# The samples' state step rebuilt and moved to blocks 1 and 2, and the state stores split into two groups

## What is computed

```python
def wkv7_scan(S0, r, w, k, v, kk, a):
    def step(S, inp):
        r_t, w_t, k_t, v_t, kk_t, a_t = inp
        sa = jnp.einsum('bhij,bhj->bhi', S, -kk_t)
        S = (S * w_t[:, :, None, :] + sa[..., None] * (kk_t * a_t)[:, :, None, :]
             + v_t[..., None] * k_t[:, :, None, :])
        return S, jnp.einsum('bhij,bhj->bhi', S, r_t)
    xs = tuple(jnp.moveaxis(t, 1, 0) for t in (r, w, k, v, kk, a))
    S, ys = lax.scan(step, S0, xs)
    return jnp.moveaxis(ys, 0, 1), S
...
    y_prompt, p_new = run_trunk(x_prompt, p_states, W, 0)      # state starts at zero
    y_sample, s_new = run_trunk(x_sample, s_states, W, PAST_LEN)  # state S0 is an input
```

## Time and profile before

| | us |
|---|---|
| median of three runs | 1320.65 (1320.16 to 1322.43) |
| the profiled execution's own time | 1319.88 |
| its span in the profile | 1318.1 |
| TensorE busy | 1212.6, 92% of the span |
| VectorE, ACT, POOL busy | 607.2, 333.7, 161.6 |
| mean granted clock of TensorE | 0.928 of full speed |

### The profile page before, as it was taken

The page is one execution under the profiler, slowest core; times in us unless marked ns, Lnnn a source line. Parts: engine busy times, 40 slices in busy tenths (PEclk is TensorE's granted clock), DMA queues, the critical chain, the costliest instruction groups (busy, mean ns, idle before and its releaser), DMA issues.

```text
span 1318.1 us, 22066 instructions
## 1 busy us (share of the span) xinstructions
PE 1212.6 (92%) x9190; PEld 1162.3 (88%) x9190; DVE 607.2 (46%) x886; ACT 333.7 (25%) x488; POOL 161.6 (12%) x134
## 2 busy tenths in 40 slices
PE   6999999999997899938789899969999999999994
PEld 6999999999997899937677758969999999999993
DVE  4443334333435768746644421466343334333445
ACT  5322122111213433102333211224221222212121
POOL 0000000000001303699700000031000000000002
PEclk9999999999998799977989856978999999999996
DMA  5222222222212022282010000212222222222211
GB/s 220 97 96 80 85 91 95 76 84 96 88 60 76 32 65 81 66 57 37 1 33 1 1 0 1 60 56 65 96 95 81 80 95 87 78 90 96 74 54 68
DMA packets 34364, 92.13 MB, mean 70 GB/s; under 512 B 10496, under 2 KB 10880, under 8 KB 34176
## 3 DMA queue, kind: packets, MB, share of 16 engines
q1 hardware_dynamic: 32576, 87.26, 22.4%
q10 hardware_dynamic: 1728, 4.03, 0.8%
HBM read 87.99 MB, written 3.28 MB: 69 GB/s over the span
## 4 chain that ended last, share of the span: by engine, by line
PE 87%; DVE 9%; DMA 1%; issue 1%; ACT 1%; ACTq 0%; SPq 0%; POOL 0%; DVEq 0%
PE ps L293 24%; PE ps L295 24%; PE ps L294 23%; DVE tb L424 2%; PE ps L781 2%; PE ps L780 1%; DMA raw<-in_w_out 1%; DVE xl L385 1%; PE ps L756 1%; PE ps L772 1%; PE ps L315 1%; PE ps L817 1%; PE ps L824 1%; PE ps L309 1%; DVE tb L416 1%
## 5 line engine op out<-in xcount | busy, mean ns | idle before, releaser
L293 PE MATMUL ps<-xh,wh 128*128 128x272 f32 x1840 | 544.0, 296 | 32.5 <-DVE xl L385 31.0
L295 PE MATMUL ps<-xh,wl 128*128 128x272 f32 x1840 | 538.5, 293 | 0.0
L294 PE MATMUL ps<-xl,wh 128*128 128x272 f32 x1840 | 536.5, 292 | 0.0
L293 PEld LDWEIGHTS ps<-xh,wh 128*128 128x128 f32 x1840 | 352.6, 192 | 38.3 <-issue 13.6
L294 PEld LDWEIGHTS ps<-xl,wh 128*128 128x128 f32 x1840 | 353.7, 192 | 0.2
L295 PEld LDWEIGHTS ps<-xh,wl 128*128 128x128 f32 x1840 | 352.8, 192 | 0.0
L272 ACT ACTIVATE wh<-raw 128x1024 fp32r<-128x1024 f32 (+1 forms) x163 | 167.7, 1032 | 354.5 <-PE ps L295 268.4
L277 DVE TENSOR_TENSOR wl<-raw,wh 128x1024 fp32r<-128x1024 f32 (+1 forms) x163 | 194.4, 1214 | 65.1 <-ACT wh L272 65.0
L295 PE MATMUL ps<-hh,wl 128*128 128x272 f32 x704 | 202.8, 288 | 0.0
L293 PE MATMUL ps<-hh,wh 128*128 128x272 f32 x704 | 202.7, 288 | 0.0
L294 PE MATMUL ps<-hl,wh 128*128 128x272 f32 x704 | 202.1, 287 | 0.0
(11 more groups left out here) (286 smaller groups left out, 1014.7 us busy)
## 6 DMA issues: line engine op xcount, KB each, us to landing
raw<-in_w_gu SPq DMA_DIRECT2D x88, 512.0 KB, 3.7
raw<-in_w_d SPq DMA_DIRECT2D x32, 512.0 KB, 3.6
raw<-in_w_in SPq DMA_DIRECT2D x19, 512.0 KB, 3.6
raw<-in_w_d SPq DMA_DIRECT2D x16, 384.0 KB, 3.0
raw<-in_w_out SPq DMA_DIRECT2D x8, 512.0 KB, 3.6
x<-in_x ACTq DMA_DIRECT2D x8, 272.0 KB, 6.8
out_y<-x SPq DMA_DIRECT2D x8, 272.0 KB, 2.1
con<-in_con ACTq DMA_DIRECT2D x1, 1094.5 KB, 9.0
```

What stands on the lines that cost most here:

```text
L293: pe.matmul(out[:, n], wh[:, s, j], right_h[:, j, col], start=opens and j == order[0], stop=False)
L294: pe.matmul(out[:, n], wh[:, s, j], right_l[:, j, col], start=False, stop=False)
L295: last = pe.matmul(out[:, n], wl[:, s, j], right_h[:, j, col], start=False, stop=closes and j == order[-1])
```

## The change

Three parts. (1) SP issues `o_shift` and `o_d` right after the load of tile 12, counted by `out_d`; then come the other loads and the first four output weights, and only then `o_a`, counted by `out_a`. Before the blocks VectorE and ACT wait for `out_d`; for `out_a` they wait in block 0, ahead of stages 16 and 17. (2) The samples: a new `q3` applies the known state to the samples' vectors (32 products of one state with 8 columns); its result enters `q7` and the outputs in `q9`. `x0` to `x3` are then one matmul each over 64 rows, and the new state is that plus the decayed old state, on VectorE. The steps `s0`, `s1` and `y` are gone. (3) The table: `w2`, `w3` go to block 0, `q0` to `q9`, `x0`, `x1` to block 1, `x2`, `x3` and `y0` to `y3` to block 2, B's norm two stages forward in block 3, and its silu, which stood in `s0`, to stage 14. Every second `fill` has two taps.

```diff
@@ mixer_sp
             for m in range(NIN):
                 load(sp, MIX0, 0, m, a["w_in"][m], KD)
-            sp.wait_ge(S("so"), 1)
-            sp.dma_start(o["o_shift"], ...).then_inc(S("out_r"), 16)
+                if m == DD1 + 4:
+                    sp.wait_ge(S("so"), 1)
+                    sp.dma_start(o["o_shift"], ...).then_inc(S("out_d"), 16)
+                    in_out(sp, DD1)
+                    ds_ = db[:, :, 527:].rearrange("p i (b c) -> p i b c", c=19)
+                    for i in range(2):
+                        sp.dma_start(o["o_d"][:, i, 0:15], db[:, i, 512:527]).then_inc(S("out_d"), 16)
+                        sp.dma_start(o["o_d"][:, i, 15:]..., ds_[:, i, :, 4:]).then_inc(S("out_d"), 16)
+            for m in range(4):
+                load(sp, MIX0, 0, OUT0 + m, a["w_out"][m], KD)
             sp.wait_ge(S("au"), 2)
             us = ub[:, :, 514:].rearrange("p i (b c) -> p i b c", c=6)
             for i in range(2):
-                sp.dma_start(o["o_a"]..., ).then_inc(S("out_r"), 16)
...
-            for m in range(4):
-                load(sp, MIX0, 0, OUT0 + m, a["w_out"][m], KD)
-            sp.wait_ge(S("out_r"), OUT_R * 16)
+                sp.dma_start(o["o_a"]..., ).then_inc(S("out_a"), 16)
...
+            sp.wait_ge(S("out_d"), OUT_D * 16)
+            sp.wait_ge(S("out_a"), OUT_A * 16)
             sp.wait_ge(S("diff"), 2)
             sp.dma_start(s0t[:], a["s0"]).then_inc(S("in_s0"), 16)
@@ wkv_act, ahead of stage 17; wkv_dve, ahead of stage 16
+            if t == 0:
+                act.wait_ge(S("out_a"), OUT_A * 16)
@@
-        BESIDE = {(1, 3): "y0", (1, 5): "y1", (1, 7): "y2", (1, 9): "y3", (1, 11): "w2", (1, 13): "w3",
-                  (2, 4): "q0", (2, 5): "q1", (2, 7): "q2", (2, 9): "q3", (2, 11): "q4", (2, 13): "q5", (2, 14): "q6",
-                  (2, 16): "q7", (2, 18): "q8", (3, 7): "b_mean", (3, 9): "b_var", (3, 11): "b_root",
-                  (3, 14): "x0", (3, 15): "x1", (3, 16): "x2", (3, 17): "x3", (3, 18): "s0", (3, 19): "s1"}
+        BESIDE = {(0, 9): "w2", (0, 11): "w3",
+                  (1, 3): "q0", (1, 4): "q1", (1, 5): "q2", (1, 6): "q3", (1, 7): "q4", (1, 9): "q5", (1, 11): "q6",
+                  (1, 12): "q7", (1, 14): "q8", (1, 16): "q9", (1, 18): "x0", (1, 19): "x1", (2, 4): "x2", (2, 6): "x3",
+                  (2, 8): "y0", (2, 10): "y1", (2, 12): "y2", (2, 14): "y3",
+                  (3, 5): "b_mean", (3, 7): "b_var", (3, 9): "b_root", (3, 14): "b_silu"}
@@ q_pe
                 if step == "q3":
+                    pe.wait_ge(S("in_s0"), 16)
                     for h in range(2):
+                        for n in range(NB):
+                            own = slice(NP_ + NT * n, NP_ + NT * n + NT)
+                            last = pe.matmul(b[hp[h], 0:2 * NS]...[:, :, NT * n:NT * n + NT],
+                                             s0t[hp[h], p, n], ar[hp[h], p, :, own], start=True, stop=True)
...
             if step[0] == "x":
                 p, h = divmod(int(step[1]), 2)
-                pe.wait_ge(S("b_norm"), 2)
-                pe.wait_ge(S("b_rec"), 1)
                 pe.wait_ge(S("ex"), 2 * p + h + 1)
-                pe.matmul(b9[hp[h], 0:NB * C], qtu[0:NS, p, h, 0:C], ex3[h][2][0:NS], start=True, stop=True)
-                pe.matmul(out, qbkv[0:NS, p, 1, C * h:C * h + C], ex3[h][0][0:NS], start=True, stop=False)
-                pe.matmul(out, qbkv[0:NS, p, 2, C * h:C * h + C], ex3[h][1][0:NS], start=False, stop=False).then_inc(S("ex_used"), 1)
+                last = pe.matmul(b[hp[h], 0:NB * C], qbkv[0:2 * NS, p, 1, C * h:C * h + C], ex[2 * p + h][0:2 * NS], start=True, stop=True)
@@ q_dve
+                if step == ("x1", "x3")[p]:
+                    wait_q(dve, 10, p)
                     for n in range(NB):
-                        last = dve.scalar_tensor_tensor(smt[:, p, n], C_("idc", C), pend[:, p, NC_ + n:NC_ + n + 1],
-                                                        qbank(9, p)[:, C * n:C * n + C], MUL, ADD)
+                        last = dve.scalar_tensor_tensor(s1t[:, p, n], s0t[:, p, n], pend[:, p, NC_ + n:NC_ + n + 1],
+                                                        qbank(10, p)[:, C * n:C * n + C], MUL, ADD)
...
+            if step in ("q7", "q9"):
+                p = 0 if step == "q7" else 1
+                for h in range(2):
+                    spread_samples(dve, 2 * p + h, slice(NS, 2 * NS), qbkv[NS:2 * NS, p, 0, C * h:C * h + C], "q0")
+            if step in ("q9", "x1"):
+                p = 0 if step == "q9" else 1
+                for h in range(2):
+                    spread_samples(dve, 2 * p + h, slice(0, NS), qtu[0:NS, p, C * h:C * h + C], "q8").then_inc(S("ex"), 1)
@@ mixer_pe, after the blocks
             for t in range(4):
                 wkv_pe(pe, t, beside)
-            q_pe(pe, "y")
...
-            pe.wait_ge(S("q_s1"), 2)
-            pe.wait_ge(S("q_y"), 2)
+            pe.wait_ge(S("q9"), 2)
+            pe.wait_ge(S("q10"), 2)
+            pe.wait_ge(S("b_norm"), 2)
@@ mixer_act, mixer_dve
-            act.wait_ge(S("out_r"), OUT_R * 16)
+            act.wait_ge(S("out_d"), OUT_D * 16)
-                for _ in range(2 if fills % 3 == 0 else 1):
+                for _ in range(2 if fills % 2 == 0 else 1):
```

More of the change, by code:

```diff
@@ L592, in in_pair @@
             return 2 if m == 2 else m % 2
-        OUT_R = 9
+        OUT_D, OUT_A = 5, 4
         OUT0 = NIN
@@ L633, in mixer_sp @@
             for i in range(2):
[L634 to L640, removed]
-            for m in range(4):
-                load(sp, MIX0, 0, OUT0 + m, a["w_out"][m], KD)
-            sp.wait_ge(S("out_r"), OUT_R * 16)
+                sp.dma_start(o["o_a"][:, i, 0:2], ub[:, i, 512:514]).then_inc(S("out_a"), 16)
+                sp.dma_start(o["o_a"][:, i, 2:].rearrange("p (b c) -> p b c", c=2), us[:, i, :, 4:]).then_inc(S("out_a"), 16)
+            sp.wait_ge(S("out_d"), OUT_D * 16)
+            sp.wait_ge(S("out_a"), OUT_A * 16)
             sp.wait_ge(S("diff"), 2)
@@ L939, in wkv_dve @@
                 beside(t, s)
+            if t == 0:
+                dve.wait_ge(S("out_a"), OUT_A * 16)
             for p in range(2):
@@ L982, in q_pe @@
                     b = job(0, p)
-                    for k, src in enumerate((v[:, p], bh[:, p], kh[:, p], ar[:, p, 0])):
-                        last = pe.transpose(b[0:NS, P * k:P * k + P], src[:, DT], ident)
+                    for k, src in enumerate((v[:, p], bh[:, p])):
+                        pe.transpose(b[0:NS, P * k:P * k + P], src[:, DT], ident)
+                    for k, src in enumerate((v[:, p], kh[:, p])):
+                        last = pe.matmul(b[NS:2 * NS, P * k:P * k + P], src[:, DT], ident, start=True, stop=True)
                     last.then_inc(S("q_job"), 1)
@@ L1009, in q_pe @@
                     for h in range(2):
-                        last = pe.matmul(b[0:NS, NS * h:NS * h + NS], qxx[0:NS, p, h], qtt[0:NS, p, 1, h], start=True, stop=True)
+                        last = pe.matmul(b[0:NS, NS * h:NS * h + NS], qnlv[0:NS, 1, p, h], qtt[0:NS, p, 0, h], start=True, stop=True)
                     last.then_inc(S("q_job"), 1)
@@ L1030, in q_pe @@
                     for h in range(2):
-                        last = pe.matmul(b[hp[h], 0:NS], qtu[0:NS, p, h, 0:C], qnrb[0:NS, p, h, 1], start=True, stop=True)
+                        last = pe.matmul(b[0:NS, C * h:C * h + C], qtt[0:NS, p, 1, h], qrhs[0:NS, p, C * h:C * h + C],
+                                         start=True, stop=True)
+                    last.then_inc(S("q_job"), 1)
+                if step == "q9":
+                    b = job(9, p)
+                    pe.wait_ge(S("q8"), p + 1)
+                    for h in range(2):
+                        out = b[hp[h], 0:NS]
+                        pe.matmul(out, qtu[0:NS, p, C * h:C * h + C], qnrb[0:NS, p, h, 1], start=True, stop=False)
+                        last = pe.matmul(out, qbkv[0:NS, p, 0, C * h:C * h + C], qakr[0:NS, p, h, 1], start=False, stop=True)
                     last.then_inc(S("q_job"), 1)
@@ L1035, in q_pe @@
                 p, h = divmod(int(step[1]), 2)
-                b9, b10 = job(9, p), job(10, p)
-                pe.wait_ge(S("b_norm"), 2)
-                pe.wait_ge(S("b_rec"), 1)
+                b = job(10, p)
                 pe.wait_ge(S("ex"), 2 * p + h + 1)
-                out = b10[hp[h], 0:NB * C]
-                pe.matmul(b9[hp[h], 0:NB * C], qtu[0:NS, p, h, 0:C], ex3[h][2][0:NS], start=True, stop=True)
-                pe.matmul(out, qbkv[0:NS, p, 1, C * h:C * h + C], ex3[h][0][0:NS], start=True, stop=False)
-                pe.matmul(out, qbkv[0:NS, p, 2, C * h:C * h + C], ex3[h][1][0:NS], start=False, stop=False).then_inc(S("ex_used"), 1)
[L1044 to L1065, removed]
+                last = pe.matmul(b[hp[h], 0:NB * C], qbkv[0:2 * NS, p, 1, C * h:C * h + C], ex[2 * p + h][0:2 * NS], start=True, stop=True)
+                if h:
```

(5 more changed lines are left out.)

121 lines of the change are left out of this document (54 added, 67 removed).

## The result

The changed kernel takes 1277.91 us (median of four runs, 1275.50 to 1279.30) against 1320.72 for the kernel before beside it: 0.9672 of its time, 95% interval 0.9652 to 0.9692. The profiled execution took 1279.23 us. Of the runs further down, two of the five executions of the stores alone took 1323.4 and 1324.3 us at a lower granted clock, and its ratio is that of the other three. New are L1008 (`q3`) and L1059 (`x`), and L1088 is the silu in its new place.

The account below looks back on a forecast made before the run. Bounds: TensorE's 22.4 us idle before block 0, behind late load 19, and block 3's end with the samples' steps at half clock. Gains and costs summed to -45.8 us, giving 1275 us on the median, range 1255 to 1295.

Parts of the forecast that it names:

- The front: Ahead of block 0: with the stores out of the way TensorE starts at 576.1 instead of 593.72, -17.6 us.
- The third rival: Ahead of the blocks: stores hold load 13 by ring order, TensorE stalls 2.7 us for it, 1278 us; chance 0.07.
- The end of block 3: Stage 14 to C's norm: samples' steps gone, clock kept at 1.00, -42.3 us; smaller terms -1.5, -1.8 and +1.4.
- C's norm: Its first matmuls (L1293 before) run at full clock, 1.85 instead of 3.96 us: -2.1 us.
- the silu stands in ACT's queue between stages 14 and 15: Block 3: the moved silu delays the chain by its 1.39 us on ACT, +1.4 us, 0 to 2.7.
- an upper bound at half clock: End of block 3: if the clock is half there, the 14.1 us become up to 28.2 and the 2.1 are lost.
- `w2` and `w3`: Both weight splits now stand inside rounds, where before one stood on block 1's chain: +4 us, 2 to 7.
- a warmer clock after the shorter wait: Block 0: after under 5 us without work instead of 22, the clock may fall later or not, -2 us, -5 to 0.
- the terms for TensorE, VectorE, POOL and the clock: Blocks 1 and 2: new matmuls +7.6, VectorE's spreads and steps +3, POOL's overlap +1.5, one clock fall +4 us.
- Rival 1: Blocks: more new work hidden, q3, VectorE's steps and POOL's overlap cost nothing, no clock fall; 1261 us, chance 0.15.
- One short fall of the clock: Block 1: q3 and the narrow x let the clock fall once, briefly, +4 us, 0 to 12.
- rivals 2 and 4: Half clock through block 2, 1295 us, chance 0.13; or from q3 in block 1 to C's norm, 1351 us, 0.03.

Follow-up runs that it names:

- the stores alone: The kernel before with only part (1), the earlier o_shift and o_d stores: 1305.98 us, 0.987 of the kernel before.
- the stores in thirds: The changed kernel with each of the two large o_d stores issued as three with 20-byte runs instead of 60: 1277.04 us, 0.967 of the kernel before.
- one state: The changed kernel with q3's 32 products of 8 columns made 4 of sample 0's state by 64 columns: 1274.61 us, 0.9656 of the kernel before.
- the samples alone: The changed kernel with the nine stores back in their old place: 1293.06 us, 0.9776 of the kernel before.

## Why the prediction was right, and where not

1275 was forecast and 1277.9 measured. The mechanism of both parts stands; the gains in three stretches and the loss in one all came out smaller than forecast, and one term was wrong in kind.

**The front (-17.6, measured -15.9).** Right. The wait is ended by `leave`, 4.2 us against "about 5"; the stores alone give 15.4. The step that was a little off is VectorE's own backlog: its split of tile 19 begins at 571.81 and not at 569.4. Over the executions of this study with the same front that split begins between 569.3 and 572.3 and block 0 between 575.4 and 578.4, around the forecast 576.1. What moves it was not tried.

**The third rival (stores hold load 13).** Its rule is borne out by the run with the stores in thirds, its price is not. In the changed kernel the load takes 5.7 us instead of the 3.6 of the earlier trace rows, the slack holds both, and TensorE has no wait for it. Taking 0 was right.

**The end of block 3 (-44.2, measured -37.3; C's norm -2.1, measured +0.1).** The failed step is "the silu stands in ACT's queue between stages 14 and 15, 1.39 us: +1.4, 0 to 2.7", with "if the clock stays at 1.00". The silu carries a table load of its own, 1.28 us. It stood in the timeline of before directly ahead of the silu of the earlier trace rows, and I read only the silu:

```profile
787.71 1.28 ACT L1092 ACT_TABLE_LOAD   x1
```

(The Trainium skill, "ScalarE activation tables: per-element evaluation and per-set limits", section "What a function is on this engine", has two functions of different sets one table load of 1283 ns apart; the 1.28 us here agree.) Between `rhs` and `tu`, where stage 16 waits, the two make 752.16 - 749.19 = 3.0 us. The clock then falls and does not return: stages 16 to 19 take 16.0 us, against 716.10 - 706.14 = 10.0 in block 2, and C's norm starts at half clock. Moving the silu gave 13.0 us, 10.6 of them in these rows. With the silu late block 3 up to C's norm takes 760.26 - 715.76 = 44.5 us, 45.3 less than before, and the forecast without the silu's +1.4 was -45.6; L1286 at 2.10 is what the term -2.1 had assumed. The sum had priced the delay and not what the delay does to the clock; an upper bound at half clock was named for these stages, but tied to nothing that I had forecast.

**Blocks 0 to 2 (+18.1, measured +12.4).** Too much in the sum.

- `w2` and `w3`: +4 forecast, net of the one split on block 1's chain before; 5.7 measured by moving them, for block 0 alone. With them the clock fell at 604 us, without them it did not, and block 0 takes 1.3 us less than before. What block 1 gained by losing its split, and the fall at 664 to 672 behind it, no run shows by itself; it may be a part of what makes blocks 1 and 2 cheaper than the sum. The forecast -2 for a warmer clock after the shorter wait is hardly borne out: block 0 runs at 0.50 from 577.9 to about 593 (windows above), 15 us, where before it ran at 0.50 from 593.7 to about 610, 16 us.
- Blocks 1 and 2 took +4.5 and +3.8, 8.3 us, where the terms for TensorE, VectorE, POOL and the clock made 16.1. The failed step is that these were summed. `q3` took 3.5 us (forecast 2.9 to 5.9) and the clock fell behind it as forecast. But the run with one state shows VectorE's taps and samples' steps come up as soon as `q3` is gone: the two lie beside each other, and one of them costs. This is shown for the stretch of `q3`; for `x` and `q9` it is argued. Rival 1, more of it hidden, was thus in part true.
- One short fall of the clock was forecast in block 1, as new. There are two there, and one in block 2; but two stood in block 1 before as well, so not all of this is new. Each lasted some 6 to 10 us and then ended under the rounds, so rivals 2 and 4, half clock from there on, did not occur.

The two errors, 9.1 us too hopeful behind stage 14 of block 3 (6.9 and 2.2) and 5.7 too careful in the blocks, partly cancel; with 1.7 at the front the span is 1277.5 instead of 1272.3. The total was nearer than its parts, and that is luck.

## What to carry to other kernels

Price a step put on a chain by all that its engine issues for it, the table load included, and then ask what the wait does to TensorE's clock up to the next dense work: here 2.7 us of ACT cost 10.6 us by the rows, and a move by four stages gained 13.0. Work beside a loop belongs where the engine that issues it isn't the one the chain waits for: the same two weight splits cost 5.7 us in the inversion's rounds and about nothing beside the TensorE stages, where block 0 was no longer than in the kernel before, which had none there. Costs on two engines that lie beside each other are not summed, as at `q3`; the longer one is taken, and the shorter is what appears when the longer is removed. And compare with what a stretch loses, here a split and a fall of the clock in block 1, not only with what it gets.

## What the runs showed of the hardware

- The clock fell at 641 us in block 1 with TensorE shown busy throughout, behind 64 instructions of 8 columns in 3.5 us, and stayed at 1.00 when these were 8 instructions of 64 columns in 0.45 us. So a fall came without idle time that the profile shows. The same 64 instructions did not bring one in the trace of the samples alone (1.00 from 656 to 676 us).
- A fallen clock was back within some 6 to 16 us under the rounds; under stages 16 to 19 of block 3 it stayed at 0.50 for some 15 us to C's norm, although TensorE was marked busy for 4.00 of 4.00 us in those windows, and with the silu late the same stages ran at 1.00. The stages alone do not decide it: in block 1 of the kernel before the clock came back under them (0.58 at 668 to 672 us, then 1.00).
- A wait of 4.2 us left block 0 about as cold as one of 22.4 us: 15 and 16 us at 0.50 behind it (13 to 16 over the traces with the shorter wait).
- Stores with runs of 20 instead of 60 bytes delay a load behind them in the same queue by 5.9 us more. This was seen for one pair of stores, and no price per run follows from it alone.

Left open, and not tried: what silu and table load would cost each by itself on the chain, whether a wait of 2.3 us without either would let the clock fall, what block 1 gained by losing `w2` and `w3`, and whether fills with two taps at every third call would change the rounds.
